# The first down period of an MLP in another order on two engines, on one Trainium2 core

## The chip, the cores and the metric

The kernel runs on 1 core of one Trainium2 chip. The metric is device time in microseconds (us). The engines are named as in the profile: PE is TensorE (PEld its weight loads), DVE is VectorE, ACT is ScalarE, POOL is GpSimd, SP is SyncE, whose queue issues most transfers.

## The reference, cut to what matters

One decoder layer over 512 tokens of width 2048, all in float32:

```python
y = mla_mixer(h, ...)                       # latent attention
h = layer_norm(ALPHA * h + y, g0, b0)
h = layer_norm(ALPHA * h + square(relu(h @ w1)) @ w2, g1, b1)   # w1: 2048x8192, w2: 8192x2048
```

The change lies at the seam between the two matrix products of the MLP: the end of `h @ w1` (up) and the start of the product with `w2` (down).

## The kernel before, in words

**Precision.** Every float32 operand is split into a high part (a copy rounded to fp32r, made by ACT) and a low part (the operand less the high part, made by DVE). A product is three matmuls: high by high, high by low, low by high (`product`, L1580 to L1585).

**Seven products for eight.** Both halves of the MLP use a Strassen-Winograd scheme: a 2x2 block product made of 7 block products, called steps here, at the price of sums of blocks. The up half has 32 pairs (the first two done in the plain way), the down half 16 periods. Pair 31 is followed at once by down period 0. In a down period, step s = 0 to 6 multiplies seven forms of the activations, read back from HBM (`down_act`, 1 MB a step, shared by two periods), by seven forms of the weights: B11, B21, T2, T1, T3, B22, T4, where T3 = B22 - B12, T1 = B12 - B11 (in period 0 it is computed as B22 - B11), T2 = T3 + B11 and T4 = B21 - T2. The T blocks overwrite their sources: T2 lies in `d_b11`, T1 in `d_b12`, T4 in `d_b21`.

**Units.** Each step has two halves, so a period has 14 units of 12 matmuls on PE (unit n = 2s, 2s + 1). For each unit ACT makes the high part (`down_weights`, L904) into one of four slots of `w_hi`, then DVE makes the low part (`down_rest`, L1312) into `w_lo`. A slot is free once PE has done the unit that used it before (`DOWN_SLOT`, `LAST_OF_SLOT`): unit 2 takes the slot of the last up step, units 4 to 13 mostly the slot of the unit four before them. After a step is done DVE moves or adds its two PSUM banks into `acc` (`evicts`, L1369 copy or L1372 add).

**The orders are written out by hand.** Each engine runs its instructions in program order and waits on semaphores. What sets the order round the change:

- DVE, end of pair 31: `c_block(31, 2)` (L1227), low parts of step 0 (`down_rest(0, 0)`), T3 (L1325), low parts of step 1 (`down_rest(0, 1)`), T2 (L1347), then `period(0)`: evicts of step 0, low parts of step 2, T1 (L1338), `hidden_sums(31)` (four short operations, L1232 to L1237), evicts 1, low parts 3, `hidden_lo(31)` (L1244), T4 (L1355), evicts 2, low parts 4, evicts 3, low parts 5, T3 of period 1, evicts 4, low parts 6, T1 of period 1 (L1333), evicts 5, low parts of step 0 of period 1. `period(1)` begins with evicts 6 of period 0, low parts 1, T2, evicts 0.
- ACT: units 0 to 3, then relu and square of the last pair's rows, units 4 and 5, `hidden_hi(31)` (L747), the store of the high rows, units 6 and 7, the store of the low rows, units 8 on. The seven rows of pair 31 (three of them made by `hidden_sums`) are the last part of the activations of chunk 7, which only periods 14 and 15 read.
- SP: the queue that issues all loads of the down half, in the order of the `sp` block (L344 to L431). The second B22 buffer, `d_b22_1`, lies at 120 KB over the rows `h_hi` that the last store reads, so its load for period 1 waits for `h_stored`, all stores of rows. Behind it on the queue stand the loads of B12 for period 1 (which wait for low parts 3 of period 0), of the two rows of LayerNorm gains and biases, `ln_rows` (L409, 1 MB each as broadcast over the partitions), and of B11 and B21 for period 1.
- POOL, from period 3 on: it multiplies and biases a piece of the residual per period (L478, L484) with `ln_rows`; DVE adds that piece to `acc` in the next period (L1382). The pieces' loads are issued on SP at the end of periods 2 to 9.
- PE: waits for the low part of each unit, for the evicts that free its banks and for the activations, and for nothing else.

Of the kernel before, what the change touches and what calls it, by code (L numbers as in the profile page):

```python
# [102 lines left out]
def mla_mlp_program(nc, xT, x, w, w_up, w_down, const, gain, ln, out):  # L103
# [3 lines left out]
    with ExitStack() as ctx:  # L107
# [90 lines left out]
        ln_rows = sb("ln_rows", [P, 2, D], at=base)  # L198
# [3 lines left out]
        d_t3, d_b22_1 = sb("d_t3", [P, 2, HB], at=base + 56 * KB), sb("d_b22_1", [P, 2, HB], at=base + 120 * KB)  # L202
# [70 lines left out]
        def _(sp):  # L273
# [99 lines left out]
            sp.wait_ge(up_unit, up_steps(last, 1))  # L373
            first_acts((2,))
# [6 lines left out]
            first_acts((3,))  # L381
# [4 lines left out]
            sp.wait_ge(h_stored, 32 * UP_PAIRS)  # L386
            load_down(d_b22[1], 1, 2, d_b22_loaded[1])

            for q in range(PERIODS):
# [17 lines left out]
                if q == 0:  # L407
                    for i in range(2):
                        sp.dma_start(ln_rows[:, i, :], ln[i].partition_broadcast(P)).then_inc(first_gains_loaded, 16)  # L409
# [18 lines left out]
                if q == RESIDUAL_FROM + 2 * TT + 1:  # L428
                    sp.wait_ge(residual_added, 2 * TT)
                    for i in range(2):  # L430
                        sp.dma_start(ln_rows[:, i, :], ln[2 + i].partition_broadcast(P)).then_inc(last_gains_loaded, 16)  # L431
# [17 lines left out]
        def _(pool):  # L449
# [22 lines left out]
            def gain_residual(r):  # L472

                part, cols = residual_part(r)
                pool.wait_ge(residual_loaded[r % 2], 16 * (r // 2 + 1))
                if r == 0:
                    pool.wait_ge(first_gains_loaded, 32)
                pool.tensor_tensor(part, part, ln_rows[:, 0, cols], ALU.mult).then_inc(residual_gained, 1)  # L478

            def bias_residual(r):  # L480

                part, cols = residual_part(r)
                pool.wait_ge(residual_gained, r + 1)
                pool.tensor_tensor(part, part, ln_rows[:, 1, cols], ALU.add).then_inc(residual_biased, 1)  # L484
# [8 lines left out]
            for t in range(TT):  # L493
                for i in range(CG if t < TT - 1 else 2):
                    part = slice(PIECE * i, PIECE * i + PIECE)
                    pool.wait_ge(gained, CG * t + i + 1)
                    pool.tensor_tensor(acc[:, t, part], acc[:, t, part], ln_rows[:, 1, part], ALU.add).then_inc(out_made[t], 1)  # L497
# [3 lines left out]
        def _(act):  # L501
# [379 lines left out]
            def spread_ln(row, part, b):  # L881


                act.activation(bank[:, b, :], ln_rows[:, row, PIECE * part:PIECE * part + PIECE], ACT.Copy)\
                    .then_inc(ln_spread, 1)
# [29 lines left out]
            down_weights(0, 4)  # L915
            down_weights(0, 5)
            hidden_hi(last)
            store_hidden(last, 0)
            down_weights(0, 6)
            down_weights(0, 7)  # L920
            store_hidden(last, 1)
            for q in range(PERIODS):
                for n in range(8 if q == 0 else 0, UNITS):
                    down_weights(q, n)
                    if q == PERIODS - 1 and n == 9:
                        act.wait_ge(last_gains_loaded, 32)
                        act.wait_ge(evicted, DOWN_EVICTS * q + 4)
                        for i in range(CG):
                            spread_ln(0, i, 2 + i)
# [22 lines left out]
        def _(dve):  # L952
# [440 lines left out]
            def period(q):  # L1393
# [3 lines left out]
                if q:  # L1397
# [5 lines left out]
                    down_t2(q)  # L1403
                    if 0 <= r < 2 * TT:
# [6 lines left out]
                if q == 0:  # L1411
                    down_t1(0)
                    hidden_sums(UP_PAIRS - 1)
# [4 lines left out]
                if q == 0:  # L1418
                    hidden_lo(UP_PAIRS - 1)
                down_t4(q)  # L1420
# [3 lines left out]
                down_rest(q, 4)  # L1424
                evicts(q, 3)
# [87 lines left out]
            for i in range(PLAIN, UP_PAIRS):  # L1513
# [22 lines left out]
                else:  # L1536
                    c_block(i, 2)
                    down_rest(0, 0)
                    down_t3(0)
                    down_rest(0, 1)  # L1540
# [543 lines left out]
```

## Time and profile before

| | |
|---|---|
| time before, median of 3 runs | 1891.42 us (1889.41 to 1900.57) |
| the profiled execution, its own time | 1892.82 us |
| its span (first to last instruction) | 1890.7 us |
| outside the span | 2.1 us |
| PE busy | 1837.9 us (97% of the span) |
| DVE busy | 1366.3 us (72%) |
| ACT busy | 889.1 us (47%) |
| POOL busy | 282.9 us (15%) |
| granted TensorE clock, mean | 0.991 of full |

The kernel spends nearly its whole span in matmuls, so what matters is the few places where PE stands still. Down period 0 begins 1236.7 us after the start of the span. All times in rows are us from the start of the span. In a timeline, "x2" merges two like instructions in a row, and the bracket is the idle time before the row and what ended it. "issue" means that the engine waited for nothing that the profile shows. In a timeline a row's length can overlap the next row by about 0.1 us, so the pitch from start to start is what an instruction costs.

### The profile page before, as it was taken

How to read it: one execution, taken by the hardware profiler on the slowest of the kernel's cores; microseconds unless marked ns; L12 is line 12 of the kernel's file. 1: busy time of each engine (PE TensorE's matmuls, PEld its weight loads, DVE VectorE, ACT ScalarE, POOL GpSimd, SP SyncE). 2: the span in 40 equal slices, each digit the busy share in tenths (PEclk: the TensorE clock that was granted, in tenths of full speed). 3: DMA queues.
4: the chain of work that ended last, by engine and by line, in shares of the span. 5: the costliest groups of instructions: out<-in, count | busy, mean ns of one | idle time of the engine just before them, and what ended most of it. 6: DMA issues, size and time to landing. Idle time of an engine off the chain costs nothing.

```text
span 1890.7 us, 28438 instructions
## 1 busy us (share of the span) xinstructions
PE 1837.9 (97%) x11120; PEld 1647.0 (87%) x11120; DVE 1366.3 (72%) x1680; ACT 889.1 (47%) x1136; POOL 282.9 (15%) x118
## 2 busy tenths in 40 slices
PE   8999999999999999999999999989999999999994
PEld 6889898988888999999999999977887888788883
DVE  3054545521128888888888888878999999999997
ACT  5255655532217656656656556533433334333434
POOL 5342232324431000000000000000111122100003
PEclk9999999999999999999999999999999999999998
DMA  6222111133234564564564554686465564654812
GB/s 225 79 80 77 56 67 55 67 138 107 100 139 147 172 223 172 195 221 167 200 216 167 206 210 167 221 317 265 174 236 202 196 254 179 234 221 170 319 67 89
DMA packets 112719, 321.30 MB, mean 170 GB/s; under 512 B 7184, under 2 KB 64656, under 8 KB 95760
## 3 DMA queue, kind: packets, MB, share of 16 engines
q1 hardware_dynamic: 53280, 256.92, 36.2%
q10 hardware_dynamic: 59376, 63.59, 10.1%
q8 instruction: 32, 0.52, 0.1%
q14 instruction: 31, 0.25, 0.0%
HBM read 253.38 MB, written 67.11 MB: 170 GB/s over the span
## 4 chain that ended last, share of the span: by engine, by line
PE 86%; DVE 7%; issue 3%; DMA 1%; ACT 1%; POOL 1%; SPq 0%; POOLq 0%; ACTq 0%; DVEq 0%
PE bank L1580 28%; PE bank L1584 28%; PE bank L1585 28%; DVE w_lo L1312 2%; DMA d_b<-down_weights 1%; DVE acc L1372 1%; PE bank L1726 1%; DVE d_b L1347 1%; POOL w_lo L453 0%; DVE acc L1382 0%; PE bank L1612 0%; POOL acc L497 0%; ACT acc L935 0%; PE bank L1821 0%; PE bank L1718 0%
## 5 line engine op out<-in xcount | busy, mean ns | idle before, releaser
L1580 PE MATMUL bank<-up_hi,w_hi 128*128 128x256 f32 x1808 | 512.6, 284 | 3.2 <-DVE w_lo L1190 2.8
L1584 PE MATMUL bank<-up_lo,w_hi 128*128 128x256 f32 x1808 | 512.3, 283 | 0.0
L1585 PE MATMUL bank<-up_hi,w_lo 128*128 128x256 f32 x1808 | 512.3, 283 | 0.0
L1580 PE MATMUL bank<-w_hi,down_act 128*128 128x512 f32 x896 | 352.0, 393 | 13.6 <-DVE w_lo L1312 5.9
L904 ACT ACTIVATE w_hi<-d_b 128x1024 fp32r<-128x1024 f32 x192 | 201.5, 1060 | 321.8 <-PE bank L1585 251.9
L1580 PEld LDWEIGHTS bank<-up_hi,w_hi 128*128 128x128 f32 x1808 | 347.6, 192 | 3.9 <-DVE w_lo L1190 3.3
L1584 PE MATMUL bank<-w_lo,down_act 128*128 128x512 f32 x896 | 350.0, 391 | 0.0
L1585 PE MATMUL bank<-w_hi,down_act 128*128 128x512 f32 x896 | 349.9, 390 | 0.0
L1585 PEld LDWEIGHTS bank<-up_hi,w_lo 128*128 128x128 f32 x1808 | 347.8, 192 | 0.0
L1584 PEld LDWEIGHTS bank<-up_lo,w_hi 128*128 128x128 f32 x1808 | 347.8, 192 | 0.0
L1312 DVE TENSOR_TENSOR w_lo<-d_b,w_hi 128x1024 fp32r<-128x1024 f32 x190 | 251.7, 1359 | 24.1 <-ACT w_hi L904 24.1
L701 ACT ACTIVATE w_hi<-up_b 128x1024 fp32r<-128x1024 f32 x180 | 187.0, 1054 | 159.4 <-PE bank L1585 131.7
L453 POOL TENSOR_TENSOR w_lo<-raw,w_hi 128x1024 fp32r<-128x1024 f32 x82 | 198.0, 2417 | 355.5 <-ACT w_hi L510 355.3
L1580 PEld LDWEIGHTS bank<-w_hi,down_act 128*128 128x128 f32 x896 | 169.0, 189 | 56.8 <-issue 14.5
L1184 DVE TENSOR_TENSOR w_lo<-up_b,w_hi 128x1024 fp32r<-128x1024 f32 x180 | 216.9, 1218 | 1.4 <-ACT w_hi L701 1.4
L1585 PEld LDWEIGHTS bank<-w_hi,down_act 128*128 128x128 f32 x896 | 168.9, 189 | 35.4
L1584 PEld LDWEIGHTS bank<-w_lo,down_act 128*128 128x128 f32 x896 | 168.9, 189 | 34.2
L478 POOL TENSOR_TENSOR residual<-residual,ln_rows 128x1024 f32<-128x1024 f32 x8 | 36.2, 4525 | 1002.4 <-DMA residual<-rows_kept 1002.4
L510 ACT ACTIVATE w_hi<-raw 128x1024 fp32r<-128x1024 f32 x82 | 86.7, 1058 | 148.2 <-PE bank L1580 115.6
L1372 DVE TENSOR_TENSOR acc<-acc,bank 128x512 f32<-128x512 f32 x202 | 130.0, 679 | 12.4 <-PE bank L1585 12.1
L1138 DVE SCALAR_TENSOR_TENSOR rows<-rows,bank 128x512 f32<-128x512 f32 x16 | 11.0, 686 | 136.5 <-PE bank L1585 136.5
L1580 PE MATMUL bank<-w_hi,act_hi 128*128 128x512 f32 x256 | 99.9, 390 | 0.0
(168 smaller groups left out, 2782.0 us busy)
## 6 DMA issues: line engine op xcount, KB each, us to landing
up_b<-up_weights SPq DMA_DIRECT2D x128, 512.0 KB, 4.8
d_b<-down_weights SPq DMA_DIRECT2D x64, 1024.0 KB, 5.3
down_act<-acts_kept SPq DMA_DIRECT2D x56, 1024.0 KB, 5.0
raw<-weights SPq DMA_DIRECT2D x82, 512.0 KB, 3.2
acts_kept<-h_hi ACTq DMA_DIRECT2D x32, 896.0 KB, 5.8
acts_kept<-h_lo ACTq DMA_DIRECT2D x32, 896.0 KB, 6.6
x_raw<-x_t SPq DMA_DIRECT2D x8, 512.0 KB, 7.7
rows<-x_rows ACTq DMA_DIRECT2D x4, 1024.0 KB, 7.9
```

What stands on the lines that cost most here:

```text
L453: pool.tensor_tensor(w_lo[:, s, :], raw[:, s % RAWS, :], w_hi[:, s, :].bitcast(f32), ALU.subtract)\
L478: pool.tensor_tensor(part, part, ln_rows[:, 0, cols], ALU.mult).then_inc(residual_gained, 1)
L510: act.activation(w_hi[:, s, :], raw[:, s % RAWS, :], ACT.Copy).then_inc(w_hi_made, 1)
L701: act.activation(w_hi[:, UP_SLOT[u], :], source[:, :], ACT.Copy).then_inc(up_hi, 1)
L904: act.activation(w_hi[:, DOWN_SLOT[n], :], source[:, ab, :], ACT.Copy).then_inc(down_hi, 1)
L1184: dve.tensor_tensor(w_lo[:, s, :], source[:, :], w_hi[:, s, :].bitcast(f32), ALU.subtract).then_inc(up_lo, 1)
L1312: dve.tensor_tensor(w_lo[:, DOWN_SLOT[n], :], source[:, ab, :], w_hi[:, DOWN_SLOT[n], :].bitcast(f32), ALU.subtract).then_inc(made, 1)
L1347: dve.tensor_tensor(d_b11[:, ab, :], d_t3[:, ab, :], d_b11[:, ab, :], ALU.add).then_inc(down_t_made, 1)
L1372: dve.tensor_tensor(part, part, of, ALU.add).then_inc(evicted, 1)
L1580: first_pass = pe.matmul(out_, a_hi, b_hi, start=start, stop=False, skip_group_check=more)
L1584: pe.matmul(out_, a_hi, b_lo, start=False, stop=False, skip_group_check=more)
L1585: return pe.matmul(out_, a_lo, b_hi, start=False, stop=stop, skip_group_check=more)
```

## The change

Three things are changed, and no instruction is added or removed.

1. **Buffers.** `d_b22_1` moves from 120 KB to 0 KB. The one tile `ln_rows` becomes two, at 8 KB and at 120 KB (where `d_b22_1` was).
2. **SP's order.** The activations of step 2 are loaded behind B12, B21 and B22 of period 0 instead of ahead of them. B22 of period 1 no longer waits for the stores of rows, only (through the queue) for the last up step. The two loads of `ln_rows`, with the wait for the stores, move from period 0 to period 1, behind the load of B12 for period 2.
3. **DVE's and ACT's order.** On DVE the low parts of step 1 come ahead of T3; `hidden_sums` moves from behind T1 to behind low parts 4, T4 with it; `hidden_lo` moves to period 1, behind T2. On ACT units 6 to 10 come ahead of `hidden_hi` and the store of the high rows, and the store of the low rows comes behind unit 5 of period 1.

```diff
-        ln_rows = sb("ln_rows", [P, 2, D], at=base)
+        ln_rows = [sb(f"ln_rows{i}", [P, D], at=base + (8, 120)[i] * KB) for i in range(2)]
...
-        d_t3, d_b22_1 = sb("d_t3", [P, 2, HB], at=base + 56 * KB), sb("d_b22_1", [P, 2, HB], at=base + 120 * KB)
+        d_t3, d_b22_1 = sb("d_t3", [P, 2, HB], at=base + 56 * KB), sb("d_b22_1", [P, 2, HB], at=base)
...
@@ SP @@
             first_acts((0, 1))
-            sp.wait_ge(up_unit, up_steps(last, 1))
-            first_acts((2,))
             sp.wait_ge(up_lo, up_parts(last, 4))
             load_down(d_b12, 0, 1, d_b12_loaded)
             sp.wait_ge(up_t_made, 4 * (last - PLAIN) + 4)
             sp.wait_ge(up_lo, up_parts(last, 6))
             load_down(d_b21, 0, 3, d_b21_loaded)
             load_down(d_b22[0], 0, 2, d_b22_loaded[0])
-            first_acts((3,))
+            sp.wait_ge(up_unit, up_steps(last, 1))
+            first_acts((2, 3))
             sp.wait_ge(up_unit, up_steps(last, 3))
             first_acts((4,))
             sp.wait_ge(up_unit, up_steps(last, 6))
             first_acts((5, 6))
-            sp.wait_ge(h_stored, 32 * UP_PAIRS)
             load_down(d_b22[1], 1, 2, d_b22_loaded[1])
...
-                if q == 0:
+                if q == 1:
+                    sp.wait_ge(h_stored, 32 * UP_PAIRS)
                     for i in range(2):
-                        sp.dma_start(ln_rows[:, i, :], ln[i].partition_broadcast(P)).then_inc(first_gains_loaded, 16)
+                        sp.dma_start(ln_rows[i][:, :], ln[i].partition_broadcast(P)).then_inc(first_gains_loaded, 16)
...
@@ ACT @@
-            down_weights(0, 4)
-            down_weights(0, 5)
+            for n in range(4, 11):
+                down_weights(0, n)
             hidden_hi(last)
             store_hidden(last, 0)
-            down_weights(0, 6)
-            down_weights(0, 7)
-            store_hidden(last, 1)
             for q in range(PERIODS):
-                for n in range(8 if q == 0 else 0, UNITS):
+                for n in range(11 if q == 0 else 0, UNITS):
                     down_weights(q, n)
+                    if q == 1 and n == 5:
+                        store_hidden(last, 1)
...
@@ DVE, period(q) @@
                     down_t2(q)
+                    if q == 1:
+                        hidden_lo(UP_PAIRS - 1)
...
                 if q == 0:
                     down_t1(0)
-                    hidden_sums(UP_PAIRS - 1)
                 evicts(q, 1)
...
                 down_rest(q, 3)
-                if q == 0:
-                    hidden_lo(UP_PAIRS - 1)
-                down_t4(q)
+                if q:
+                    down_t4(q)
                 evicts(q, 2)
...
                 down_rest(q, 4)
+                if q == 0:
+                    hidden_sums(UP_PAIRS - 1)
+                    down_t4(0)
                 evicts(q, 3)
...
@@ DVE, end of pair 31 @@
                     down_rest(0, 0)
+                    down_rest(0, 1)
                     down_t3(0)
-                    down_rest(0, 1)
                     down_t2(0)
```

The other lines of the diff (L478, L484, L431, L497, L884) only name `ln_rows[0]` and `ln_rows[1]` where they named the two rows of the one tile.

## Rows read from the trace of the kernel before

**Rows 1.** The chain that ended last, 1228 to 1286 us: start us, us, what.

```profile
1229.48 10.14 DMA d_b<-down_weights
...
1253.33 0.44 DVE hidden L1237
1253.79 1.71 ACT h_hi L747
...
1259.43 1.94 DVE h_lo L1244
...
1267.47 12.70 DMA d_b<-down_weights
```

**Rows 2.** Timeline of PE: start us, us, instruction [idle before, what ended it].

```profile
1236.68 0.40 PE L1580 MATMUL bank<-w_hi,down_act 128*128 128x512 f32 x1
...
1243.24 0.47 PE L1580 MATMUL bank<-w_hi,down_act 128*128 128x512 f32 x1 [0.93 <-issue]
...
1258.40 0.76 PE L1580 MATMUL bank<-w_hi,down_act 128*128 128x512 f32 x1 [3.70 <-issue]
1258.96 0.63 PE L1584 MATMUL bank<-w_lo,down_act 128*128 128x512 f32 x1
1259.39 0.63 PE L1585 MATMUL bank<-w_hi,down_act 128*128 128x512 f32 x1
...
1284.94 0.50 PE L1580 MATMUL bank<-w_hi,down_act 128*128 128x512 f32 x1 [1.63 <-DVE w_lo L1312]
```

**Rows 3.** Busy time by stretch (count), granted clock, DMA share, GB/s.

```profile
1284.94:1323.00 38.06, 38.06 (x168) 31.53 (x169) 34.19 (x37) 13.41 (x13) 0.00 (x0) 1.00 0.63 237
...
1445.00:1483.50 38.50, 35.69 (x149) 28.71 (x149) 34.60 (x37) 14.51 (x14) 0.24 (x1) 0.96 0.67 250
```

**Rows 4.** Timeline of DVE, end of pair 31 to period 1.

```profile
1234.35 2.35 DVE L1312 TENSOR_TENSOR w_lo<-d_b,w_hi 128x1024 fp32r<-128x1024 f32 x2
...
1241.92 2.35 DVE L1312 TENSOR_TENSOR w_lo<-d_b,w_hi 128x1024 fp32r<-128x1024 f32 x2
1244.19 2.36 DVE L1347 TENSOR_TENSOR d_b<-d_t,d_b 128x1024 f32<-128x1024 f32 x2
1246.46 1.28 DVE L1369 COPY acc<-bank 128x512 f32<-128x512 f32 x2
1247.66 2.35 DVE L1312 TENSOR_TENSOR w_lo<-d_b,w_hi 128x1024 fp32r<-128x1024 f32 x2
...
1252.20 0.42 DVE L1232 TENSOR_TENSOR hidden<-hidden 128x256 f32<-128x256 f32 x1
...
1272.80 2.36 DVE L1325 TENSOR_TENSOR d_t<-d_b,d_b 128x1024 f32<-128x1024 f32 x2 [1.35 <-DMA d_b<-down_weights]
...
1280.20 2.36 DVE L1333 TENSOR_TENSOR d_b<-d_b,d_b 128x1024 f32<-128x1024 f32 x2 [1.57 <-DMA d_b<-down_weights]
...
1310.91 1.23 DVE L1312 TENSOR_TENSOR w_lo<-d_b,w_hi 128x1024 fp32r<-128x1024 f32 x1 [2.05 <-ACT w_hi L904]
```

**Rows 5.** Timeline of ACT, unit 2 and 3 of period 0.

```profile
1236.94 2.01 ACT L904 ACTIVATE w_hi<-d_b 128x1024 fp32r<-128x1024 f32 x2 [1.81 <-PE bank L1585]
```

**Rows 6.** Timeline of SP's queue, which issues the loads.

```profile
1265.46 0.81 SPq L356 DMA_DIRECT2D d_b<-down_weights  x2
```

**Rows 7.** Queries on one transfer: B21 for period 1 (issued at 1278.71).

```profile
DMA to landing us min/median/max: 4.9/4.9/4.9
```

**Rows 8.** The same for the store of pair 30's low rows (issued 1224.10).

```profile
DMA to landing us min/median/max: 28.1/28.1/28.1
```

**Rows 9.** Timeline of POOL, two of the eight residual pieces.

```profile
1439.50 2.40 POOL L478 TENSOR_TENSOR residual<-residual,ln_rows 128x1024 f32<-128x1024 f32 x1 [27.25 <-DMA residual<-rows_kept]
...
1521.46 8.04 POOL L478 TENSOR_TENSOR residual<-residual,ln_rows 128x1024 f32<-128x1024 f32 x1 [27.37 <-DMA residual<-rows_kept]
```

**Rows 10.** Timeline of DVE beside the first of those two.

```profile
1439.60 6.72 DVE L1312 TENSOR_TENSOR w_lo<-d_b,w_hi 128x1024 fp32r<-128x1024 f32 x2
```

**Rows 11.** Timeline of PE just after it.

```profile
1452.19 0.63 PE L1580 MATMUL bank<-w_hi,down_act 128*128 128x512 f32 x1 [2.80 <-DVE w_lo L1312]
```

More of the change, by code:

```diff
@@ L430, in _ @@
                     for i in range(2):
-                        sp.dma_start(ln_rows[:, i, :], ln[2 + i].partition_broadcast(P)).then_inc(last_gains_loaded, 16)
+                        sp.dma_start(ln_rows[i][:, :], ln[2 + i].partition_broadcast(P)).then_inc(last_gains_loaded, 16)
             def store_piece(t, i):
@@ L477, in gain_residual @@
                     pool.wait_ge(first_gains_loaded, 32)
-                pool.tensor_tensor(part, part, ln_rows[:, 0, cols], ALU.mult).then_inc(residual_gained, 1)
+                pool.tensor_tensor(part, part, ln_rows[0][:, cols], ALU.mult).then_inc(residual_gained, 1)
             def bias_residual(r):
@@ L483, in bias_residual @@
                 pool.wait_ge(residual_gained, r + 1)
-                pool.tensor_tensor(part, part, ln_rows[:, 1, cols], ALU.add).then_inc(residual_biased, 1)
+                pool.tensor_tensor(part, part, ln_rows[1][:, cols], ALU.add).then_inc(residual_biased, 1)
             for q in range(PERIODS):
@@ L496, in _ @@
                     pool.wait_ge(gained, CG * t + i + 1)
-                    pool.tensor_tensor(acc[:, t, part], acc[:, t, part], ln_rows[:, 1, part], ALU.add).then_inc(out_made[t], 1)
+                    pool.tensor_tensor(acc[:, t, part], acc[:, t, part], ln_rows[1][:, part], ALU.add).then_inc(out_made[t], 1)
         @block.scalar
@@ L881, in spread_ln @@
             def spread_ln(row, part, b):
-                act.activation(bank[:, b, :], ln_rows[:, row, PIECE * part:PIECE * part + PIECE], ACT.Copy)\
+                act.activation(bank[:, b, :], ln_rows[row][:, PIECE * part:PIECE * part + PIECE], ACT.Copy)\
                     .then_inc(ln_spread, 1)
```

## The prediction

> **What bounds the kernel now.** I read the page first: PE is busy for 97% of the span, so only time in which PE stands still can be won, plus the slow matmuls that follow a long stop. The change touches the first two down periods, so I measured those. From the first down matmul to the first of period 1 PE took 1284.94 - 1236.68 = 48.26 us [rows 2]. The next period, with no stop in it, is 168 matmuls in 38.06 us [rows 3]: 0.2265 us a matmul, 2.72 us a unit of twelve. **Period 0 therefore loses 10.2 us**, and that is all there is to win here.
>
> The timeline of PE says where. Unit 2 was due at 1236.68 + 2 x 2.72 = 1242.1 and began at 1243.24: 1.1 lost. Before unit 6 PE stood for 3.70 us and then ran at 0.43 us a matmul (1258.96 to 1259.39) instead of 0.2265, the lower of its two clock levels, for some seven matmuls: 3.7 + 7 x 0.2 = 5.1 with both. Before period 1 it stood for 1.63 [rows 2]. The remaining 2.4 us are stops of under a microsecond before units 4, 8 and 12 and restarts. That the clock fell behind a stop of 3.70 us is a row; by the Trainium skill (TensorE: Matmul & The Clock Gate, What's actually happening) a stopped array falls to 1.2 GHz, which agrees with the doubled pitch.
>
> The chain of waits gives the reasons. (a) DVE waited for B22 of period 0, which took 10.14 us to come, did T3, and only then the low parts of step 1, although ACT had made their high parts by 1236.94 + 2.01 = 1238.95 [rows 1, 5]. (b) Before unit 6 ACT stood in `hidden_hi` (1.71 us, begun 1253.79), which waits for the sums that end at 1253.77; its high part for unit 6 stood behind that [rows 1]. (c) The load of B22 for period 1 and everything behind it on SP's queue waited for the stores of rows and were issued at 1265.46 [rows 6]. Five megabytes then came at once, so T3 of period 1 waited 1.35 us and T1 of period 1, for a B11 that took 12.70 us, another 1.57 [rows 1, 4].
>
> **The change step by step.** It moves work and adds none, so I walk DVE, the busiest of the helpers, through the new order with pitches from its rows. A pair of 128x1024 operations (low parts or a T) costs 2.27 (1241.92 to 1244.19 to 1246.46), a pair of evicts 1.20 (1246.46 to 1247.66) [rows 4]; `hidden_sums` 1.57 (1252.20 to 1253.77), `hidden_lo` 1.94 [rows 1, 4]. PE begins a unit 1.32 after DVE begins its pair (1241.92 to 1243.24) [rows 2, 4].
>
> Low parts 0 begin at 1234.35 as before and end at 1236.6. Low parts 1 can start when ACT has unit 2, at about 1237.95, and end at 1240.25; PE could have unit 2 at 1239.3 and wants it at 1242.1. **Stop before unit 2 gone: 1.1.** B22 of period 0 lands by 1239.62 (issue 1229.48 plus 10.14 [rows 1]), and sooner if anything, because the load of one set of activations now stands behind it; so T3 runs at 1240.25 without a wait, T2 at 1242.5, evicts 0 at 1244.8, low parts 2 at 1246.0. PE can have unit 4 at 1247.3 and wants it at 1247.55. T1 1248.3, evicts 1 1250.5, low parts 3 1251.7, unit 6 ready at 1253.05 and due at 1253.0. ACT's unit 6 now comes right behind T1 (first half done 1249.4), not behind `hidden_hi`. **The stop of 3.70 and its slow matmuls are gone: 5.1**, with perhaps 0.1 left. Evicts 2 1254.0, low parts 4 1255.2, unit 8 ready 1256.5, due 1258.5. Sums 1257.5, T4 1259.0, evicts 3 1261.3, low parts 5 1262.5, unit 10 ready 1263.8, due 1264.0. T3 of period 1 1264.8, evicts 4 1267.0, low parts 6 1268.2, unit 12 ready 1269.55, due 1269.4. T1 of period 1 1270.5, evicts 5 1272.8, low parts 0 of period 1 1274.0, so period 1 begins at 1275.3 against 1274.9 due: 0.4. Then evicts 6, low parts 1, T2, `hidden_lo`, evicts 0, low parts 2 add 1.20 + 2.27 + 2.27 + 1.94 + 1.20 from 1276.3, and unit 4 of period 1 is ready at 1286.5 against 1286.2 due: 0.3. From there DVE gains 4 us a period on PE, as it did before: at 1310.91 it already waited 2.05 us for ACT, which waited for PE [rows 4]. The 2 us of `hidden_lo` are paid out of that.
>
> **What stays** is 0.1 + 0.1 + 0.4 + 0.3, about 0.9 us with restarts. The sum: 10.2 - 0.9 = **9.3 us off**, with every later period shifted as a whole.
>
> **What the moved work could cost.** The order fits only if the transfers keep up. B12 of period 1 is issued behind low parts 3, at 1254.0, and T3 wants it at 1264.8; B11 behind T4, at 1261.3, and T1 wants it at 1270.5; B21 behind low parts 6, at 1270.5, and low parts 1 want it at 1277.4 (ACT one microsecond sooner). The nearest rows are 4.9 us for a load with little beside it and 12.70 with four others ahead [rows 1, 7]. At 4.9 they land at 1258.9, 1266.2 and 1275.4, all in time; at 12.70 B12 would be 1.9 late, B11 3.5 and B21 about 6. I take 4.9, because the queue ahead is empty: with the `ln_rows` loads and B22 out of the way each of the three has at most one store or load beside it. `ln_rows` moves to period 1, where 2 MB stand ahead of activations 2 and B11 for period 2. Before, the last of five transfers landed at 1267.47 + 12.70 = 1280.17, which is 14.7 us after the first was issued, under 3 us each [rows 1, 6]. Behind low parts 3 of period 1, at 1291, the same five-deep queue lands B11 at 1305.7; T1 of period 2 comes one period after the last, 1270.5 + 38.06 = 1308.6: hidden, by some 3 us. On ACT the late `hidden_hi` (1259.1 to 1260.8) lies between unit 10 and unit 11, whose slot is free only when unit 8 is done, at 1253.05 + 3 x 2.72 = 1261.2: nothing. It also needs the stores of pair 30. The slowest took 28.1 us and landed at 1252.2 [rows 8], beside seven megabytes of loads, and B22's load puts one more in its way, under 3 us; 1255 is well ahead of 1259.1. The store of the low rows, behind unit 5 of period 1, holds ACT for under 1 us and its 4 us of slack cover it. If that slack were gone it would show as a later unit 6.
>
> **Rivals.**
>
> *A transfer takes the place of the removed waits.* For it: that is what the trace has now, twice. Against it: the queue is emptied ahead of each. If B11 for period 1, or B11 for period 2 behind `ln_rows`, comes 3.5 us late, PE stops as long and restarts slowly as at 1258.40, 1.5 more: 5 us of the 9.3 are lost, the time is 1887.
>
> *The port race ends on the other side, slower.* In the even periods 2 to 8 a residual piece lands just as DVE goes from an evict to a low part. POOL's multiply begun at 1439.50, 0.1 us ahead of DVE's pair, ran in 2.40 us, and the pair took 6.72 instead of 2.35; PE stopped for 2.80 us and slowed down. The piece at 1521.46 lost the race: it stretched to 8.04 us, so there it was POOL that waited, and POOL's time is not on the path [rows 9 to 11]. The stretch round the lost race has 149 matmuls in 38.50 us where 170 fit: 4.8 us [rows 3]. By the Trainium skill (SBUF — State Buffer, SBUF: two separate sides) whichever of a DVE and a GpSimd operation on SBUF starts first holds the shared port for its whole length; the trace agrees with both lengths. A shift of everything by 9 us can retune a race that turns on 0.1 us. It decides the sign if DVE loses all four and not one: 3 x 4.8 - 9.3 = 5.1 us slower, 1896.5. For it: the margin is thin. Against it: piece and low part both hang on the same DVE instruction half a period earlier, so their distance should not move.
>
> *DVE wins all four races* besides: 4.8 more off, 1877.3.
>
> **How the numbers follow.** The profiled execution took 1892.82 us, 1.4 above the median of 1891.42 and well inside the runs. Its sum is 1892.82 - 9.3 = 1883.5; from the median it is **1882.1 us**, my number. Chances: the forecast with its small errors 0.72, a late transfer 0.14, all races won 0.08, three or more lost 0.06. The range takes in the won races at the low end (1877, less 0.5 for what I left standing) and the late transfer and one more lost race at the high end (1887 to 1889): 1876.5 to 1889. This kernel's measurement tells about 1% from no change, 19 us, and the whole loss in these periods is 10.2, so within 1% holds nearly all: faster 0.02, same 0.96, slower 0.02.
>
> **What would show it.** Right: unit 2 at 1242.1, unit 6 at 1253.1 with no slow matmuls behind it, period 1 at about 1275.3, no DVE wait for a transfer in T3 and T1 of period 1, and period 4 on 9.3 us earlier. Wrong: a DVE wait for `d_b` in front of L1325 or L1333, a stop of over 1 us before period 1 or its unit 4, or a POOL multiply of 2.4 us with a DVE pair of 6.7 in more than one even period. The forecast fails if PE, rather than starting earlier, waits at period 2 for low parts behind a late B11.

## The result, and the profile after

| | before | after |
|---|---|---|
| first comparison, median | 1893.11 us (6 runs, 1889.41 to 1900.57) | 1883.73 us (6 runs, 1881.81 to 1885.08) |
| ratio after to before, 95% interval | | 0.9945 [0.9929, 0.9962] |
| second comparison, on another occasion | 1895.31 us (14 runs) | 1883.77 us (8 runs), 0.9943 [0.9917, 0.997] |
| profiled execution, span | 1892.82, 1890.7 us | 1885.08, 1882.9 us |

The forecast was 1882.1 us, 9.3 less than the median of 1891.42 that stood then. The measured time is 1883.73, and with more runs of the kernel before its median moved up to 1893.11: the difference is 9.4 us, half a per cent and within the 1% forecast as "same". The interval of the ratio stands for 7.2 to 13.4 us, and the second comparison gives 11.5, so that the medians meet the forecast to 0.1 us is luck; what confirms it is the count below. One run of the kernel before, beside the first four experiments, took 4695.44 us and is left out there.

All further numbers in this document lean on one ledger, a count of lost time by period. Every kernel issues the same 2688 matmuls in the down half. I add up the distance from start to start of neighbouring ones, less 0.2267 us each, and get what a period loses. Periods are counted from 0. "0 and 1" is what the change is about; "3 to 10" are the periods in which POOL works on a residual piece.

| profiled execution | first down matmul at | periods 0 and 1 | period 3 | period 5 | periods 3 to 10 |
|---|---|---|---|---|---|
| before | 1236.7 | 10.3 | 0.0 | 5.0 | 8.8 |
| after | 1240.5 | 0.9 | 2.2 | 0.6 | 6.7 |

The spans differ by 7.8 us: 9.4 from periods 0 and 1, 2.2 from periods 3 to 10, less 3.8 by which the down half began later in this execution of the kernel after. Those 3.8 us are there long before the lines that differ: the 701st matmul of the program begins at 157.5 us before and at 161.3 after. In the twelve profiled executions of this study the first down matmul lies anywhere from 1235.5 to 1240.5. The three earliest (1235.5, 1236.7, 1237.2) belong to the three kernels that keep DVE's and ACT's order of before; with one profile of each kernel that may be chance, and no run here settles it.

The busy times of the two down periods of after, from the first matmul of period 0, of period 1 and on. The columns are those of [rows 3].

```profile
1240.45:1279.01 38.56, 38.56 (x170) 31.20 (x168) 37.14 (x43) 18.44 (x18) 0.00 (x0) 1.00 0.79 305
1279.01:1317.60 38.59, 38.59 (x170) 31.63 (x170) 36.17 (x38) 14.78 (x14) 0.00 (x0) 1.00 0.83 324
```

Each takes 38.6 us where an undisturbed one takes 38.06 and period 0 took 48.26; PE is busy in all of it and the granted clock is 1.00. PE at the three places of [rows 2]:

```profile
1240.45 0.40 PE L1581 MATMUL bank<-w_hi,down_act 128*128 128x512 f32 x1
...
1245.69 0.39 PE L1586 MATMUL bank<-w_hi,down_act 128*128 128x512 f32 x1
1245.92 0.39 PE L1581 MATMUL bank<-w_hi,down_act 128*128 128x512 f32 x1
...
1278.68 0.39 PE L1586 MATMUL bank<-w_hi,down_act 128*128 128x512 f32 x1
1279.01 0.50 PE L1581 MATMUL bank<-w_hi,down_act 128*128 128x512 f32 x1
```

Period 0 begins at 1240.45. Unit 2 begins at 1245.92, 0.23 us behind the matmul before it, so without a stop, and period 1 at 1279.01, with 0.33 us from start to start: a tenth of a microsecond late. DVE in the new order, the counterpart of [rows 4]:

```profile
1238.11 2.35 DVE L1310 TENSOR_TENSOR w_lo<-d_b,w_hi 128x1024 fp32r<-128x1024 f32 x2
1241.84 2.36 DVE L1310 TENSOR_TENSOR w_lo<-d_b,w_hi 128x1024 fp32r<-128x1024 f32 x2 [1.38 <-ACT w_hi L903]
1244.12 2.35 DVE L1323 TENSOR_TENSOR d_t<-d_b,d_b 128x1024 f32<-128x1024 f32 x2
1246.39 2.35 DVE L1345 TENSOR_TENSOR d_b<-d_t,d_b 128x1024 f32<-128x1024 f32 x2
1248.66 1.28 DVE L1367 COPY acc<-bank 128x512 f32<-128x512 f32 x2
1249.86 2.35 DVE L1310 TENSOR_TENSOR w_lo<-d_b,w_hi 128x1024 fp32r<-128x1024 f32 x2
...
1255.59 2.35 DVE L1310 TENSOR_TENSOR w_lo<-d_b,w_hi 128x1024 fp32r<-128x1024 f32 x2
...
1262.80 2.35 DVE L1353 TENSOR_TENSOR d_b<-d_b,d_b 128x1024 f32<-128x1024 f32 x2
...
1268.54 2.35 DVE L1323 TENSOR_TENSOR d_t<-d_b,d_b 128x1024 f32<-128x1024 f32 x2
...
1274.27 2.35 DVE L1331 TENSOR_TENSOR d_b<-d_b,d_b 128x1024 f32<-128x1024 f32 x2
...
1277.74 2.36 DVE L1310 TENSOR_TENSOR w_lo<-d_b,w_hi 128x1024 fp32r<-128x1024 f32 x2
...
1305.28 1.23 DVE L1310 TENSOR_TENSOR w_lo<-d_b,w_hi 128x1024 fp32r<-128x1024 f32 x1 [2.05 <-ACT w_hi L903]
```

Shift these by the 3.77 us of the later start and lay them beside the walk: T3 1240.35 (forecast 1240.25), low parts 2 1246.1 (1246.0), low parts 3 1251.8 (1251.7), T4 1259.0 (1259.0), T3 of period 1 1264.8 (1264.8), T1 of period 1 1270.5 (1270.5), low parts of period 1 1274.0 (1274.0). No T waits for anything. The whole list of what DVE waited for in these 67 us (engine, line, what it waited for, us in total, times, longest):

```profile
DVE w_lo L1310 <- ACT w_hi L903: 3.4, 2, 2.0
DVE acc L1367 <- PE bank L1586: 0.4, 1, 0.4
```

Both waits for loads, 1.35 and 1.57 us in [rows 4], are gone, and the wait for B22 in [rows 1]. Of the two waits for ACT one is the 2.05 us of slack at 1305.28, as at 1310.91 before; the other is before unit 2, harmless, and ends on something I had not foreseen: ACT itself waited for B21, which landed at 1240.72. It began 3.81 us later than before, where PE's last up step had let it go at 1236.94 [rows 5], and the whole down half began 3.77 later, so the load cost nothing.

```profile
1240.75 2.01 ACT L903 ACTIVATE w_hi<-d_b 128x1024 fp32r<-128x1024 f32 x2 [1.85 <-DMA d_b<-down_weights]
...
1262.91 1.71 ACT L746 ACTIVATE h_hi<-hidden 128x1792 fp32r<-128x1792 f32 x1 [1.83 <-DVE hidden L1235]
```

`hidden_hi` (the second row) now stands where nothing is queued behind it that is wanted.

### The profile page after: what moved, and what is told of

It is laid out like the page before. It is cut to its first block, busy times and chain, and to the rows that moved or that the text cites. A ratio compares the mean times of both kernels' runs of the same rounds, so it can differ in the third digit from the quotient of the medians.

```text
span 1882.9 us, 28438 instructions
## 1 busy us (share of the span) xinstructions
PE 1837.8 (98%) x11120; PEld 1647.0 (87%) x11120; DVE 1365.6 (73%) x1680; ACT 890.5 (47%) x1136; POOL 283.5 (15%) x118
## 3 DMA queue, kind: packets, MB, share of 16 engines
q10 hardware_dynamic: 59376, 63.59, 10.2%
## 4 chain that ended last, share of the span: by engine, by line
PE 89%; DVE 7%; issue 3%; ACT 1%; POOL 1%; POOLq 0%; DVEq 0%; ACTq 0%
PE bank L1581 29%; PE bank L1585 29%; PE bank L1586 29%; DVE w_lo L1310 2%; DVE acc L1370 1%; PE bank L1727 1%; DVE d_b L1345 1%; POOL w_lo L452 0%; DVE acc L1380 0%; PE bank L1613 0%; POOL acc L496 0%; ACT acc L933 0%; PE bank L1822 0%; DVE d_t L1323 0%; PE bank L1719 0%
```

## The experiments

**Three parts, taken apart.** The change has a swap (low parts 1 ahead of T3), the buffers with SP's order, and the late rows (sums, high and low rows, stores, T4). The late rows need the buffers: with `d_b22_1` over the rows' buffer, SP's load for period 1 would wait for a store that comes after it. So four of the mixed versions exist, and with before and after they answer what each part is worth. All ran on one chip, 3 rounds each, with before at 1895.21 us (22 runs). Each has one profile, and the ledger of periods 0 and 1 bears that: it gives 10.3 in both profiles without the change and 0.8 or 0.9 in all six with the whole change.

*The swap alone*, on the kernel before:

```diff
                     down_rest(0, 0)
-                    down_t3(0)
                     down_rest(0, 1)
+                    down_t3(0)
                     down_t2(0)
```

> Before, with one change: the low parts of step 1 ahead of T3. The measure is what down periods 0 and 1 take over 38.06 us each: 10.3 us before, 0.9 with the whole change. The theory (DVE's chain sets PE's starts): the stop of 1.1 us before unit 2 is gone, T3 starts at the landing of B22 or 0.7 us later, and all that follows on DVE comes about 1.6 us earlier; the stop before unit 6 stays, as ACT still makes unit 6 behind the high rows, and so do the waits for B12 and B11 of period 1. Loss 8.7 us, time 1.6 us less. The rival (the next wait takes it all back): unit 2 is on time, unit 6 and period 1 come as late as before, loss 10, time unchanged.

Measured: 1893.35 us, ratio 0.9983 [0.9966, 1.0001]; loss of periods 0 and 1 8.7 us, as the theory had it. Unit 6 still waited:

```profile
1255.55 0.39 PE L1585 MATMUL bank<-w_hi,down_act 128*128 128x512 f32 x1
1259.54 0.47 PE L1580 MATMUL bank<-w_hi,down_act 128*128 128x512 f32 x1 [3.60 <-issue]
```
```profile
DVE d_b L1333 <- DMA d_b<-down_weights: 1.6, 1, 1.6
DVE d_t L1325 <- DMA d_b<-down_weights: 1.3, 1, 1.3
```

PE stands 3.60 us before unit 6 and DVE still waits 1.6 and 1.3 us for the loads of period 1. The timed ratio cannot tell 1.6 us from nothing; the ledger can. The expectation also had the stop before unit 6 unchanged, and it nearly is (3.70 before).

*Buffers and SP's order alone*: DVE and ACT as before.

```diff
-        ln_rows = sb("ln_rows", [P, 2, D], at=base)
+        ln_rows = [sb(f"ln_rows{i}", [P, D], at=base + (8, 120)[i] * KB) for i in range(2)]
-        d_b22_1 = sb("d_b22_1", [P, 2, HB], at=base + 120 * KB)
+        d_b22_1 = sb("d_b22_1", [P, 2, HB], at=base)
...
-            sp.wait_ge(h_stored, 32 * UP_PAIRS)
             load_down(d_b22[1], 1, 2, d_b22_loaded[1])
...
-                if q == 0:
+                if q == 1:
+                    sp.wait_ge(h_stored, 32 * UP_PAIRS)
                     ...
```

> Before, with the buffers moved and SP's order changed, DVE's and ACT's orders as before. The theory: DVE no longer waits for B12 and B11 of period 1 (1.35 and 1.57 us before), the stops before unit 12 and before period 1 (0.6 and 1.8 us) go, the stops before units 2 and 6 stay. Loss of periods 0 and 1 about 7.9 us against 10.3, time 2.4 us less. The rival (transfers were not what held period 1, only the late DVE chain): loss still 9.5 to 10. A second rival (this is where nearly all of the gain comes from): loss under 4.

Measured: 1891.07 us, ratio 0.9969 [0.9945, 0.9993]; loss 7.7 us, nothing of it in period 1. The theory's 7.9. (The timed 4.1 us are more than the 2.6 of the ledger, and the interval, 1.3 to 10.4 us, holds both.) PE's stops before units 2 and 6 are there (1.30 and 4.10 us from start to start). What DVE waited for:

```profile
DVE w_lo L1311 <- ACT w_hi L903: 3.0, 2, 2.1
DVE d_t L1324 <- DMA d_b<-down_weights: 2.9, 1, 2.9
```

The one wait for a load left is the 2.9 us for B22 of period 0, which this part does not touch.

*The rows back in their early places*, all else as after:

```diff
-            for n in range(4, 11):
-                down_weights(0, n)
+            down_weights(0, 4)
+            down_weights(0, 5)
             hidden_hi(last)
             store_hidden(last, 0)
+            down_weights(0, 6)
+            down_weights(0, 7)
+            store_hidden(last, 1)
...
                     down_t1(0)
+                    hidden_sums(UP_PAIRS - 1)
                 evicts(q, 1)
...
+                if q == 0:
+                    hidden_lo(UP_PAIRS - 1)
+                down_t4(q)
                 evicts(q, 2)
...
```

> The kernel after, with the last pair's rows (sums, high and low rows, their two stores, T4) back in their places of before; buffers, SP's order and the swap of step 1 and T3 stay. The theory: unit 6 waits again for ACT, which stands in the high rows: a stop of about 3.4 us there and some seven matmuls at 0.43 us; loss of periods 0 and 1 about 5.5 us, time 4.6 us more than after. The rival (with the transfers and the swap in place DVE is early enough that the rows no longer hurt): loss under 2 us.

Measured: 1891.16 us, ratio 0.9963 [0.9948, 0.9978], 7.4 us more than the 1883.77 of the kernel after on the other occasion, which was on another chip; the two ratios, 0.9963 and 0.9943, are 3.8 us apart. The ledger is sharper: loss 6.1 us against the 5.5 expected.

```profile
1253.68 1.70 ACT L746 ACTIVATE h_hi<-hidden 128x1792 fp32r<-128x1792 f32 x1 [6.14 <-DVE hidden L1236]
...
1255.88 2.00 ACT L903 ACTIVATE w_hi<-d_b 128x1024 fp32r<-128x1024 f32 x2 [0.50 <-ACT h_hi L746]
```
```profile
1256.97 2.36 DVE L1311 TENSOR_TENSOR w_lo<-d_b,w_hi 128x1024 fp32r<-128x1024 f32 x2 [2.12 <-ACT w_hi L903]
```
```profile
1258.30 0.47 PE L1579 MATMUL bank<-w_hi,down_act 128*128 128x512 f32 x1 [3.60 <-issue]
...
1259.53 0.57 PE L1584 MATMUL bank<-w_hi,down_act 128*128 128x512 f32 x1
1259.89 0.63 PE L1579 MATMUL bank<-w_hi,down_act 128*128 128x512 f32 x1
1260.32 0.63 PE L1583 MATMUL bank<-w_lo,down_act 128*128 128x512 f32 x1
```

ACT waits 6.14 us for the sums, makes the high rows, and only at 1255.88 the high part for unit 6; DVE, which has evicted by then, waits 2.12 us for it (the row in the middle), and PE stands 3.60 us. Read the last three rows: PE resumed near full pitch and slowed down only with the sixth matmul; nine were slow from there on, seven of them at 0.43 us. In [rows 2] it was slow at once and for seven. The slow stretch costs 1.7 us here and 1.4 there, but the stop before unit 8 is shorter by as much, 0.5 against 0.8, so this is not the 0.6 us by which I was off. The stop before unit 6 cost 3.8 us where I had 3.4, and the one before unit 8 stands in no expectation. The profile also loses 2.2 us more than after_again in period 15 (5.1 against 2.9), where PE waits 1.84 us for an evict and then runs slowly; nothing ties that to the place of the rows.

*The swap undone*, all else as after:

```diff
                     down_rest(0, 0)
+                    down_t3(0)
                     down_rest(0, 1)
-                    down_t3(0)
                     down_t2(0)
```

> The kernel after, with T3 again ahead of the low parts of step 1. The theory: DVE waits idle for the landing of B22 again and its whole chain through period 0 is 1.7 us later; unit 2 late by 1.1, the rest in small stops; loss of periods 0 and 1 about 2.6 us against 0.9. The rival (DVE's chain has slack behind unit 2): loss 2.0 or less, all of it before unit 2. If B22 now lands before DVE is done with step 0's low parts, the loss stays at 0.9 or 1.0.

Measured: 1887.34 us (5 runs), ratio 0.9941 [0.9911, 0.9971]; loss 2.4 us, 2.6 expected. The ratio is that of the kernel after (0.9943): only the ledger shows this difference.

```profile
1236.37 2.35 DVE L1310 TENSOR_TENSOR w_lo<-d_b,w_hi 128x1024 fp32r<-128x1024 f32 x2
1241.62 2.36 DVE L1323 TENSOR_TENSOR d_t<-d_b,d_b 128x1024 f32<-128x1024 f32 x2 [2.91 <-DMA d_b<-down_weights]
1243.90 2.35 DVE L1310 TENSOR_TENSOR w_lo<-d_b,w_hi 128x1024 fp32r<-128x1024 f32 x2
```

DVE is idle for 2.91 us before T3 although the high parts of unit 2 are there, and unit 2 is late by 1.05 us.

Put together, losses of periods 0 and 1: before 10.3, swap 8.7, buffers 7.7, swap and buffers 6.1, buffers and late rows 2.4, all three 0.9. The swap is worth 1.6, 1.6 and 1.5 whatever it is added to; the buffers 2.6; the late rows 5.3 (with the buffers alone) and 5.2. **The parts add up**, 1.6 + 2.6 + 5.2 = 9.4, and over half is the late rows. That part holds two moves that no run takes apart: the high rows behind units 6 to 10 on ACT, and the sums (1.57 us, ahead of the evicts that precede low parts 3) later on DVE. The 2.12 us for which DVE waits in rows_early is what ACT's queue adds after DVE's own delay; how the 5.2 us would divide between the two is not shown.

**The race between POOL and DVE.** This was my rival for a slower result, and the two profiles had lost it in different periods, 5 before and 3 after. In the kernel after (POOL, then DVE):

```profile
1357.01 2.41 POOL L477 TENSOR_TENSOR residual<-residual,ln_rows 128x1024 f32<-128x1024 f32 x1 [769.42 <-DMA residual<-rows_kept]
...
1436.17 8.08 POOL L477 TENSOR_TENSOR residual<-residual,ln_rows 128x1024 f32<-128x1024 f32 x1 [27.33 <-DMA residual<-rows_kept]
```
```profile
1357.17 6.66 DVE L1310 TENSOR_TENSOR w_lo<-d_b,w_hi 128x1024 fp32r<-128x1024 f32 x2
...
1436.20 2.36 DVE L1310 TENSOR_TENSOR w_lo<-d_b,w_hi 128x1024 fp32r<-128x1024 f32 x2
```

POOL first by 0.16 us: DVE's pair takes 6.66 us. POOL first by 0.03: POOL's multiply takes 8.08 and DVE's pair its 2.36. Before, 0.10 decided for POOL [rows 9, 10]. (The prediction speaks of even periods, at whose end a piece is loaded; the collision falls into the period behind, 3, 5, 7 or 9.) The 8.08 us are more than one instruction of DVE's: POOL waits through five of them that read two SBUF tiles (the pair, the addition of the piece, T2) and ends 2.37 us after the next evict begins, at 1441.88. To see whether the start really decides, I let POOL win always:

```diff
@@ SP @@
                 next_act(4)
+                residual load                      (from behind next_act(6))
                 if q < PERIODS - 1: ... load B21(q + 1)
@@ POOL @@
                 if 0 <= r < 2 * TT:
+                    pool.wait_ge(evicted, DOWN_EVICTS * (q - 1) + 13)
                     gain_residual(r)
                     bias_residual(r)
```

> The kernel after, but each residual piece is loaded earlier (ahead of the load of B21 for the next period) and POOL's multiply waits for the first of the two evicts of step 6, so that it starts 0.6 us ahead of DVE's low parts of step 1 in all eight periods 3 to 10. The theory (a DVE operation on two SBUF tiles and a POOL operation exclude each other for their whole length, and who starts first decides): the pair of low parts takes about 6 us instead of 2.35 in each of the eight periods, ahead of T2 and with no slack behind it; PE loses about 2.2 us in period 3 and 4 to 5 in each of periods 4 to 10 instead of 0.6: about 28 us more than after. The rival (the slow pair in period 5 had another cause, as the load of activations): 0.6 a period as before, time unchanged.

Measured: 1911.67 us (5 runs), ratio 1.008 [1.0055, 1.0105]. Losses: 1.9 in period 3, 4.4 to 4.7 in each of periods 4 to 10, 33.9 in all; 27.9 us more than the kernel after beside it.

```profile
1436.50 2.40 POOL L477 TENSOR_TENSOR residual<-residual,ln_rows 128x1024 f32<-128x1024 f32 x1 [37.04 <-DVE acc L1371]
1438.98 3.25 POOL L483 TENSOR_TENSOR residual<-residual,ln_rows 128x1024 f32<-128x1024 f32 x1
```
```profile
1435.74 1.28 DVE L1371 TENSOR_TENSOR acc<-acc,bank 128x512 f32<-128x512 f32 x2
1436.93 6.38 DVE L1311 TENSOR_TENSOR w_lo<-d_b,w_hi 128x1024 fp32r<-128x1024 f32 x2
```

The evicts at 1435.74 (they read PSUM and one SBUF tile) take their ordinary 1.28 us beside POOL; the pair of low parts that begins 0.43 us behind POOL takes 6.38. That is its own 2.35, the 1.97 us that were left of the multiply, and about 2.1 for the bias, which got its turn between the two low parts. Why the bias waits for one instruction of DVE's here and the late multiply above for five stays open. Then two ways to keep POOL out of the way. *The gate*:

```diff
                 if 0 <= r < 2 * TT:
+                    pool.wait_ge(down_lo_b, STEPS * q + 5)
                     gain_residual(r)
                     bias_residual(r)
```

> The kernel after, with POOL's work on each residual piece held back until DVE has made the low parts of step 4, where DVE runs ahead of PE and later waits for it anyway. The theory (the two POOL operations block DVE for some 3.3 us wherever they fall, and the price is what slack DVE has there): the race at the start of the period cannot be lost any more (2.2 us in period 3 of the profiled run of after, about 5 us in period 5 of before), and the 0.6 us in each of periods 4 to 10 falls to 0 to 0.5: 3 to 6 us less than after. The rival (DVE is over its budget in these periods, so where the block falls does not matter): still 0.6 in each, 2 us less than after at most. If the block hits unit 10 or 12, more than 1 us in each period, slower than after.

Measured: **1874.37 us** (1873.51 to 1877.24, 4 runs), ratio to before 0.9884 [0.9847, 0.992]. It loses nothing in periods 3 to 10, where the two profiles of the kernel after lose 6.7 and 7.2: better than the 3 to 6 us expected. (The medians are 9.4 us apart, from 4 and 8 runs; the spans of the two profiles taken beside each other are 6.9 apart.)

```profile
1412.24 2.41 POOL L477 TENSOR_TENSOR residual<-residual,ln_rows 128x1024 f32<-128x1024 f32 x1 [33.44 <-DVE w_lo L1311]
1414.73 3.47 POOL L483 TENSOR_TENSOR residual<-residual,ln_rows 128x1024 f32<-128x1024 f32 x1
```
```profile
1412.76 0.69 DVE L1371 TENSOR_TENSOR acc<-acc,bank 128x512 f32<-128x512 f32 x1 [0.60 <-PE bank L1587]
1414.12 0.69 DVE L1371 TENSOR_TENSOR acc<-acc,bank 128x512 f32<-128x512 f32 x1 [0.67 <-PE bank L1587]
1414.72 1.22 DVE L1311 TENSOR_TENSOR w_lo<-d_b,w_hi 128x1024 fp32r<-128x1024 f32 x1
1417.99 1.29 DVE L1311 TENSOR_TENSOR w_lo<-d_b,w_hi 128x1024 fp32r<-128x1024 f32 x1 [2.05 <-ACT w_hi L904]
```

The multiply fits in the time in which DVE waits for PE and evicts. The bias gets its turn when DVE's low part at 1414.72 is done, runs through the 2.05 us in which DVE waits for ACT, and ends 0.2 us after. DVE's next low part takes 1.29 us for 1.22. In periods 5 to 10 it is the same; in period 3 the bias comes first and DVE's pair is held up:

```profile
1376.41 2.39 POOL L483 TENSOR_TENSOR residual<-residual,ln_rows 128x1024 f32<-128x1024 f32 x1
```
```profile
1376.64 4.49 DVE L1311 TENSOR_TENSOR w_lo<-d_b,w_hi 128x1024 fp32r<-128x1024 f32 x2
```

PE loses nothing there either, since DVE has the slack. My figure of 3.3 us of blocking "wherever they fall" was wrong: it is 2.1 us in period 3 and hardly any in the others. *The halves*, each of the four 512 columns wide:

```diff
                 if 0 <= r < 2 * TT:
-                    gain_residual(r)
-                    bias_residual(r)
+                    pool.wait_ge(down_lo_b, STEPS * q + 3);   gain_residual(r, 0)
+                    pool.wait_ge(down_t_made, 8 * q + 8);     gain_residual(r, 1)
+                    pool.wait_ge(down_lo_b, STEPS * q + 5);   bias_residual(r, 0)
+                    pool.wait_ge(down_t_made, 8 * q + 10);    bias_residual(r, 1)
```

> The kernel after, with each of POOL's two operations on a residual piece cut into two halves of 512 columns, and each half held back until DVE is about to begin a pair of evicts (which read PSUM and one SBUF tile). The theory: an evict does not exclude POOL, so of each half only the 0.1 to 0.5 us that it runs past the 1.2 us of evicts blocks DVE, about 1.2 us a period instead of 3.3; the losses of periods 3 to 10 (6.6 us in the profiled run of after) fall under 1 us; 5 to 6 us less than after, the fastest of all. The rival (evicts are blocked too, or each POOL operation has a fixed cost that halving doubles): 0.6 or more stays in each period.

Measured: 1876.65 us (4 runs), 0.99 [0.9863, 0.9937]; no loss in periods 3 to 10 either. It is as good in the ledger (span 1875.2 us beside the simple gate's 1875.1). The expectation, the fastest of all, is not met: its slower median is within the spread.

> The kernel after, unchanged, beside the others on the same chip. Its down periods 0 and 1 should lose 0.9 us again, whatever periods 3 to 10 do; the theory of the race expects a loss of about 2 us in period 3 or 4 to 5 us in period 5, 7 or 9 in some of its executions and 0.6 in the other periods.

Measured: 1883.77 us (8 runs, 1878.1 to 1891.37). Periods 0 and 1 lose 0.8; period 5 loses 3.3, period 3 nothing. The race fell out another way in the same program. The 3.3 us are less than the expected 4 to 5: PE stopped for 2.76 us, in period 5 of before for 2.80, but here it went on near full pitch (its next matmul starts 0.32 us later, and not 0.43).

```profile
1445.01 0.49 PE L1581 MATMUL bank<-w_hi,down_act 128*128 128x512 f32 x1 [2.76 <-DVE w_lo L1310]
```

**Do the two losses add?** The same gate on the kernel before, against the gated kernel after, 5 rounds:

```diff
                 if 0 <= r < 2 * TT:
+                    pool.wait_ge(down_lo_b, STEPS * q + 5)
                     gain_residual(r)
                     bias_residual(r)
```

> The kernel before, with POOL's work held back until the low parts of step 4 are made, and nothing else. The theory (periods 0 and 1 and the race are separate losses that add): periods 3 to 10 lose 0 instead of 4.5 plus whatever races are lost, about 9 us in the profiled run; periods 0 and 1 lose 10.3 as before; about 1884 us, 9.4 more than the same gate on the kernel after. The rival (the race hides part of what the change gains, or the gate needs the shift of the change to work): more than 1 us is lost in periods 3 to 10, or the two gated kernels differ by under 7 or over 12 us.

Measured: 1884.56 us (11 runs, 1881.7 to 1888.77), ratio to before 0.9959 [0.9946, 0.9972].

> The kernel after with the same gate, beside the gated kernel before. The theory: 0.9 us lost in periods 0 and 1, none in periods 3 to 10, 9.4 us less than the gated kernel before, and its runs lie closer together than those of the kernels without the gate (which spread over 13 to 17 us here), because no race is left in this stretch.

Measured: 1876.82 us (6 runs, 1873.56 to 1880.3), ratio to before 0.9916 [0.9896, 0.9936]. In the ledger both lose nothing in periods 3 to 10; periods 0 and 1 lose 10.3 and 0.9. From first to last down matmul they take 1857.83 - 1235.52 = 622.3 and 1852.07 - 1238.96 = 613.1 us, 9.2 apart. The medians are 7.7 apart, in the bounds but less than 9.4; runs of one kernel here lie 7 us apart, and the down half of the gated kernel after began 3.4 us later in its profile, so I do not read the missing 1.7 us as an effect of the change, nor is it excluded (the three earliest starts of the result's section bear on it). The spreads are 7.1 and 6.7 us (11 and 6 runs) beside 11.5 of the kernel before (15 runs). That the gate narrows them is not shown: the kernel after without it spread over 3.3 us in 6 runs and over 13.3 in 8.

```profile
1430.00:1650.00 220.00, 220.00 (x973) 182.25 (x972) 202.51 (x216) 84.93 (x81) 32.24 (x12) 1.00 0.61 229
```
```profile
1430.00:1650.00 220.00, 218.54 (x956) 177.94 (x955) 215.46 (x211) 84.95 (x81) 51.57 (x12) 1.00 0.60 224
```

220 us of periods 5 to 10, the gated kernel before above, the kernel after below. DVE is busy for 202.51 us and not 215.46, POOL for 32.24 and not 51.57, for the same operations but a few at the edges: most of the difference is time in which one was held up by the other and its record ran on.

The ledger of all runs, with the first down matmul:

| kernel | first down | 0 and 1 | 3 | 5 | 3 to 10 |
|---|---|---|---|---|---|
| swap_only | 1239.4 | 8.7 | 2.2 | 4.9 | 11.0 |
| buffers_only | 1237.2 | 7.7 | 0.0 | 4.7 | 8.6 |
| rows_early | 1238.2 | 6.1 | 2.3 | 3.3 | 9.4 |
| no_swap | 1238.7 | 2.4 | 0.0 | 4.9 | 8.8 |
| after_again | 1239.1 | 0.8 | 0.0 | 3.3 | 7.2 |
| pool_wins | 1237.5 | 0.9 | 1.9 | 4.4 | 33.9 |
| pool_gate_low4 | 1239.0 | 0.9 | 0.0 | 0.0 | 0.0 |
| pool_halves | 1239.6 | 0.8 | 0.0 | 0.0 | 0.0 |
| before_gate | 1235.5 | 10.3 | 0.0 | 0.0 | 0.0 |
| after_gate | 1239.0 | 0.9 | 0.0 | 0.0 | 0.0 |

## Why the prediction was right, point by point

**The bound.** That 10.2 us could be won in these two periods and no more held: the ledger has 10.3. **The walk of DVE** was right to 0.1 us at every station named above, because DVE's durations did not change with their order here and it had no wait for a load left. The residue of 0.9 us was measured as 0.9, and at the places forecast: period 1 begins at 1275.24 and its unit 4 at 1286.38, less the later start, against 1275.3 and 1286.5. So the mechanism was right; that the timed medians differ by 9.4 us too is luck, as said above.

**The attribution** was right in kind and uneven in size. Unit 2's stop was put at 1.1 and the swap is worth 1.5 to 1.6, as it also brings DVE's later chain forward. Unit 6's stop was put at 5.1, the late rows are worth 5.2 to 5.3, which agrees in part by luck: with the stop before unit 8, which goes with them, the stop before unit 6 and its slow matmuls lose 6.1 us in before and 6.0 in rows_early, and 0.8 us of small delays, in period 0 and at the start of period 1, come in exchange. The buffers, which I never priced as a part, are worth 2.6, close to the 1.63 before period 1 with the small stops around it.

**The transfers** were the weakest step. I took 4.9 us for each of the three loads of period 1. Queries on each load of after give 5.7 us for B12 (issued 1258.02) and 4.7 for B21 (1274.44), and for B11 (1265.18):

```profile
DMA to landing us min/median/max: 7.0/7.0/7.0
```

B11 was carried beside the store of the high rows issued 0.5 us ahead of it, and landed 2.1 us before T1 wanted it, not 4.3. B11 for period 2, behind the two `ln_rows`, landed 2.7 us before its T1 (12.5 us after its issue; I had 3 us to spare). I also wrote that B22 of period 0 would land sooner if anything, with one load fewer ahead of it: it landed 3.1 us after the first down matmul, before it was 2.9. The store of pair 30's high rows landed 11 us after its issue instead of 22, so the bandwidth may have gone there, which no run shows. ACT waited 1.68 us for B21 of period 1, and its high part was ready 1 us before DVE wanted it. None of this reached PE, since what the walk needed was only that they be in time.

**The rivals.** A transfer late by 3.5 us did not occur. The race is real, and the forced version shows its mechanism; by the Trainium skill (SBUF — State Buffer, SBUF: two separate sides) the first to start of a DVE instruction with two SBUF inputs and a GpSimd one that reads SBUF holds the port for its whole length, and that agrees with 6.38 us for the pair against 2.35. The 8.04 us of [rows 9] and the 8.08 above agree with it less well: POOL's record begins no later than DVE's, by up to 0.06 us earlier in the profiles, and POOL is yet the one that waits, for five instructions of DVE's and not for one. My price of 4.8 for a lost race is right for what a period 4 to 10 then loses if PE's clock falls behind the stop (4.4 to 5.0); in rows_early and after_again it did not fall, and the period lost 3.3. Against the 0.6 that it loses anyway the race costs 2.7 to 4.4, and in period 3 it is 1.9 to 2.3, where DVE has no residual piece to add and some slack. So four lost races would have cost less than the 3 x 4.8 of the prediction, and a won one gives back less than 4.8. I also argued that the distance of piece and low part should not move; it moved by 0.1 us from one execution to the next, which is enough. I treated the 0.6 us of the other periods as fixed. It was the same contention, at a later place (in period 5 of after DVE's pair at 1443.07 takes 5.60 us), and the gate removed it: 4.5 of the 6.7 us that the kernel after lost in this stretch were of this kind, and the prediction left them standing.

**The chances.** The whole effect was 0.5%, inside the 1% that I gave 0.96.

## What to carry to other kernels

Where one engine with known durations feeds the bound, walk it through the new order instruction by instruction, starting from the real start of the stretch: the result was good to a tenth of a microsecond here, where every load was in time, so spend the doubt on the loads. An instruction that nobody wants soon (here the rows' high parts) must not stand in an in-order queue ahead of one that is wanted, least of all when it waits for a third engine. And when two engines exclude each other on a port, do not leave the start of the unhurried one to the landing of a transfer: gate it on the place where the other one has its slack; that one line was worth 6.7 to 8.8 us here in the ledger, beside 9.4 for the whole reordering.

## What the runs showed of the hardware that I had not expected

- A race decided by about 0.1 us: POOL ahead by 0.03 us (1436.17 in after) or 0.06 (its first piece before, at 1362.74, DVE at 1362.80) lost to DVE, ahead by 0.10 or 0.16 it won [rows 9, 10]. The same program lost it in period 3 in one execution (2.2 us) and in period 5 in another (3.3 where it loses 0.6 otherwise).
- A stop of 3.60 us was followed by five matmuls near the full pitch of 0.23 us before the 0.43 began, in rows_early and in swap_only, while [rows 2] were slow at once. A stop of 2.8 us in period 5 was followed by slow matmuls in before ([rows 11], granted clock 0.61 from 1452.19 to 1456.60), swap_only, buffers_only and no_swap, and not in rows_early and after_again (granted clock 1.00 from 1445.10 to 1449.10): the same stop costs 3.3 us of the period or 4.7 to 5.0. The fall once followed a stop of 1.84 us (rows_early, period 15, granted clock 0.67 from 1848.78 to 1854.00).
- POOL's bias operation shows 3.25 us in most periods, but 2.39 where it comes first and DVE waits (pool_gate_low4, 1376.41): part of a long record is waiting.
